# Two-layer decoder trunk on one core: the order of work at the changes of stage is rewritten

## The reference

```python
for l in range(DEPTH):                      # DEPTH = 2
    u = rms_norm(h, norm_pre_mix[l])
    if l == 0: mix = mamba2_mixer(u, ...)   # in_proj, conv, chunked scan, gate, out_proj
    else:      # shared K and V from rms_norm(h, kv_norm_w) @ w_k, w_v, once
               mix = diff_attention(u, k_shared, v_shared, ...)
    h = h + rms_norm(mix, norm_post_mix[l])
    m = sq_relu_mlp(rms_norm(h, norm_pre_mlp[l]), mlp_w1[l], mlp_w2[l])
    h = h + rms_norm(m, norm_post_mlp[l])
return h
```

## Time and profile before

| | us |
|---|---|
| median of 3 runs | 2575.64 (2575.22 to 2575.69) |
| the profiled execution | 2576.61 |
| its span | 2574.9 |
| TensorE busy with matmuls | 2525.8 (98%) |
| VectorE busy | 1796.9 (70%) |
| ScalarE busy | 1212.9 (47%) |
| mean granted TensorE clock | 0.997 |

### The profile page before, as it was taken

The page is one execution under the profiler, slowest core; times in us unless marked ns, Lnnn a source line. Parts: engine busy times, 40 slices in busy tenths (PEclk is TensorE's granted clock), DMA queues, the critical chain, the costliest instruction groups (busy, mean ns, idle before and its releaser), DMA issues.

```text
span 2574.9 us, 45532 instructions
## 1 busy us (share of the span) xinstructions
PE 2525.8 (98%) x17258; PEld 2324.6 (90%) x17258; DVE 1796.9 (70%) x2563; ACT 1212.9 (47%) x1580; POOL 151.9 (6%) x269
## 2 busy tenths in 40 slices
PE   6999999999999999999999999999999999999997
PEld 6999999999898989999998898998899998989896
DVE  4878777877876566666656877778866666575666
ACT  4555555554554443434434654555544434443433
POOL 2221022202100000000000000000000000000000
PEclk9999999999999999999999999999999999999999
DMA  6665665555556666665666555555565666666664
GB/s 177 197 199 164 199 191 188 179 187 181 187 167 193 189 190 192 185 193 184 196 188 193 174 183 176 175 171 165 170 187 182 197 190 190 188 192 190 189 190 135
DMA packets 266506, 474.13 MB, mean 184 GB/s; under 512 B 16577, under 2 KB 50226, under 8 KB 264626
## 3 DMA queue, kind: packets, MB, share of 16 engines
q1 hardware_dynamic: 263296, 457.76, 58.0%
q0 software_dynamic: 2624, 15.00, 1.8%
q10 hardware_dynamic: 498, 0.18, 0.0%
HBM read 470.70 MB, written 2.19 MB: 184 GB/s over the span
## 4 chain that ended last, share of the span: by engine, by line
PE 95%; DVE 3%; ACT 1%; DMA 1%; issue 0%; POOL 0%; ACTq 0%; DVEq 0%; SPq 0%; POOLq 0%
PE ps L1295 31%; PE ps L1297 30%; PE ps L1296 30%; PE ps L1475 1%; DVE h L974 0%; DVE whl L843 0%; DVE xhl L931 0%; DMA par_rows<-a_conv_b 0%; PE ps L1558 0%; PE ps L1479 0%; PE ps L1413 0%; ACT whl L588 0%; PE ps L1467 0%; DVE y L947 0%; PE ps L1379 0%
## 5 line engine op out<-in xcount | busy, mean ns | idle before, releaser
L843 DVE TENSOR_TENSOR whl<-raw,whl 128x1024 fp32r<-128x1024 f32 x865 | 1073.8, 1241 | 716.8 <-ACT whl L588 705.1
L588 ACT ACTIVATE whl<-raw 128x1024 fp32r<-128x1024 f32 x865 | 916.3, 1060 | 1206.1 <-PE ps L1297 1195.7
L1295 PE MATMUL ps<-xhl,whl 128*128 128x256 f32 (+1 forms) x3600 | 1014.4, 282 | 11.1 <-DVE xhl L931 10.1
L1297 PE MATMUL ps<-xhl,whl 128*128 128x256 f32 (+1 forms) x3600 | 1006.4, 280 | 0.0
L1296 PE MATMUL ps<-xhl,whl 128*128 128x256 f32 (+1 forms) x3600 | 1005.3, 279 | 0.0
L1295 PEld LDWEIGHTS ps<-xhl,whl 128*128 128x128 f32 (+1 forms) x3600 | 677.1, 188 | 16.9 <-DVE xhl L931 11.7
L1296 PEld LDWEIGHTS ps<-xhl,whl 128*128 128x128 f32 (+1 forms) x3600 | 677.3, 188 | 3.1 <-issue 1.9
L1297 PEld LDWEIGHTS ps<-xhl,whl 128*128 128x128 f32 (+1 forms) x3600 | 677.0, 188 | 0.0
L1295 PE MATMUL ps<-whl,bhl 128*128 128x512 f32 x1312 | 511.4, 390 | 0.0
L1296 PE MATMUL ps<-whl,bhl 128*128 128x512 f32 x1312 | 510.8, 389 | 0.0
L1297 PE MATMUL ps<-whl,bhl 128*128 128x512 f32 x1312 | 510.5, 389 | 0.0
(11 more groups left out here) (210 smaller groups left out, 1640.5 us busy)
## 6 DMA issues: line engine op xcount, KB each, us to landing
raw<-mlp_w SPq DMA_DIRECT2D x512, 512.0 KB, 4.2
raw<-a_in_proj SPq DMA_DIRECT2D x161, 512.0 KB, 4.7
raw<-a_out_proj SPq DMA_DIRECT2D x64, 512.0 KB, 4.1
raw<-b_w_q SPq DMA_DIRECT2D x32, 512.0 KB, 3.6
raw<-w_k SPq DMA_DIRECT2D x32, 512.0 KB, 3.7
raw<-w_v SPq DMA_DIRECT2D x32, 512.0 KB, 3.7
raw<-b_out_proj SPq DMA_DIRECT2D x32, 512.0 KB, 3.7
cumb<-cum_scratch POOLq DMA_DIRECT2D x8, 1024.0 KB, 7.5
```

The lines of the kernel that those rows point to most:

```text
L588: sc.activation(whi[:, s.split, lo:lo + SLAB], raw[:, s.raw, :], ACT.Copy).then_inc(hi_ready, 1)
L843: ve.tensor_tensor(out=wlo[:, s.split, lo:lo + SLAB], in0=raw[:, s.raw, :], in1=whi[:, s.split, lo:lo + SLAB].bitcast(F32), op=ALU.subtrac ...
L1295: te.matmul(outs, lh, rh, start=start, stop=False, skip_group_check=True)
L1297: return te.matmul(outs, ll, rh, start=False, stop=stop, skip_group_check=True)
```

## The change

The last slab of a stage reports its first half of tokens separately (`half_done`), and VectorE adds that half while TensorE still works on the other. The third block of y is weighed one half of the tokens at a time, the first half ahead of the norm factor, the second later. The first 256 columns of h are renewed as two pieces of 128. TensorE transposes one tile instead of four before the first slab, runs the products with the high half of x as soon as ScalarE has it (`first_slab`), and transposes the later pairs one by one, each ahead of or in the middle of a slab (`x_slab`). ScalarE takes pair 2+i ahead of the split of step i. VectorE takes pairs 1 to 3 inside `boundary`, between parts of `residual`, and pairs 4 to 7 in the steps 0 to 3, with the last block of y and the last piece of h in step 1. The keys' halves move to the steps 0, 1, 4, 5 and 6. ScalarE's squares keep their steps, 3 and 4 (6 and 7 in attention).

The constants:

```diff
-TURN_BANKS = (3, 4, 5, 6, 2, 7, 3, 4)
-H_PIECES = ((0, 256), (256, 512), (512, 1024), (1024, 1536), (1536, 2048))
+TURN_BANKS = ((3, 7), (4, 4), (5, 5), (6, 6), (2, 2), (7, 7), (3, 3), (4, 4))
+H_PIECES = ((0, 128), (128, 256), (256, 512), (512, 1024), (1024, 1536), (1536, 2048))
+X_PIECE = ((0, 1), (2, 2), (3, 3), (3, 3), (4, 4), (4, 4), (5, 5), (5, 5))
+    XK_TURNS = {0: (0,), 1: (1,), 4: (2, 3), 5: (4, 5), 6: (6, 7)}
```

ScalarE's parts:

```diff
+            def x_first(r, col):
+
+                act.wait_ge(xt_first, r)
+                x_tile(0, 0, TURN_BANKS[0], xhi, col).then_inc(x_first_hi, 1)
+                act.wait_ge(xt_done, KT // 2 * r + 1)
+                x_tile(0, 1, TURN_BANKS[0], xhi, col).then_inc(x_hi, 1)
...
                     ahead = ph.slab(first_k + k + LEAD, t, per)
+                    if early:
+                        early(unit, i)
...
                 def first_step(unit, i):
-                    if unit == "up" and i < 3:
-                        x_halves(r, range(2 * i + 2, 2 * i + 4), col)
                     if unit == "up" and i in (3, 4):
                         act.wait_ge(h_new, H_STEPS * r)
                         square_sums(r, range(4 * (i - 3), 4 * (i - 2)))
...
+                def first_turns(unit, i):
+                    if unit == "up" and i < 6:
+                        x_halves(r, (2 + i,), col)
...
-                steps(ph, 0, MLP_FIRST, first_step)
+                steps(ph, 0, MLP_FIRST, first_step, early=first_turns)
```

VectorE's parts:

```diff
             def last_output(ph, r, i):
...
                 for t, done in enumerate((half_added, acc_added)):
+                    if t == 0:
+                        dve.wait_ge(half_done, r + 1)
+                    else:
+                        dve.wait_ge(slab_used, ph.slab(ph.slabs - 1).used)
...
-            def boundary(r, slab=None, col=0):
-
-                weigh_y(r, 2)
+            def post_norm(r):
+
+                weigh_y(r, 2, (0,))
                 dve.wait_ge(y_sq, MT * NT * (r + 1))
                 link(ve.reduce_sum(sum_y, ssy, AX))
                 inverse_rms(rsy, sum_y, D, 1e-6)
+
+            def boundary(r, slab, col):
+
+                post_norm(r)
                 residual(r, 0)
                 residual(r, 1)
-                if slab:
-                    x_halves(r + 1, range(2), col)
+                dve.wait_ge(x_first_hi, r + 1)
+                x_tile(0, 0, TURN_BANKS[0], xhi, xlo, col).then_inc(x_first_lo, 1)
                 residual(r, 2)
-                if slab:
-                    split(slab)
-                residual(r, 3)
+                dve.wait_ge(x_hi, KT // 2 * (r + 1) + 1)
+                x_tile(0, 1, TURN_BANKS[0], xhi, xlo, col).then_inc(x_lo, 1)
+                residual(r, 3, (0,))
+                x_halves(r + 1, (1,), col)
+                residual(r, 3, (1,))
+                split(slab)
+                x_halves(r + 1, (2,), col)
+                weigh_y(r, 2, (1,))
+                residual(r, 4, (0,))
+                x_halves(r + 1, (3,), col)
+                residual(r, 4, (1,))
+
+            def later_pieces(r, i, col):
+
+                if i < 4:
+                    x_halves(r + 1, (4 + i,), col)
+                if i == 1:
+                    weigh_y(r, 3)
+                    residual(r, 5)
+
+            def last_norm(r):
+
+                post_norm(r)
+                for n in range(4):
+                    residual(r, n)
+                weigh_y(r, 2, (1,))
+                residual(r, 4)
                 weigh_y(r, 3)
-                residual(r, 4)
+                residual(r, 5)
...
                 def first_step(unit, i):
-                    if unit == "up" and i < 3:
-                        x_halves(r, range(2 * i + 2, 2 * i + 4), col)
+                    if unit == "up":
+                        later_pieces(r - 1, i, col)
...
             def att_step(first, g, unit, i):
                 if first and unit == "q":
-                    if i < 3:
-                        x_halves(2, range(2 * i + 2, 2 * i + 4), 16)
-                    for j in {0: (0, 1), 3: (2, 3), 4: (4, 5), 5: (6, 7)}.get(i, ()):
+                    for j in XK_TURNS.get(i, ()):
                         dve.wait_ge(xk_hi, j + 1)
                         x_half(j, TURN_BANKS[j], khi, klo, 64, xk_lo)
+                    later_pieces(1, i, 16)
```

TensorE's parts:

```diff
+            def first_slab(r, s):
+
+                transpose_x(r, 0)
+                pe.wait_ge(lo_ready, s.n + 1)
+                wh, wl = slot(s, 2)
+                outs = [ps[:, f // 2, f % 2 * S:(f % 2 + 1) * S] for f in range(4)]
+                cols = [slice(f * P, (f + 1) * P) for f in range(4)]
+                pe.wait_ge(x_first_hi, r)
+                for f in range(4):
+                    te.matmul(outs[f], wh[:, 0, cols[f]], xhi[:, 0, :], start=f % 2 == 0, stop=False, skip_group_check=True)
+                    te.matmul(outs[f], wl[:, 0, cols[f]], xhi[:, 0, :], start=False, stop=False, skip_group_check=True)
+                transpose_x(r, 1)
+                pe.wait_ge(x_first_lo, r)
+                for f in range(4):
+                    te.matmul(outs[f], wh[:, 0, cols[f]], xlo[:, 0, :], start=False, stop=False, skip_group_check=True)
+                pe.wait_ge(x_lo, KT // 2 * r + 1)
+                for f in range(4):
+                    last = three(outs[f], (wh[:, 1, cols[f]], wl[:, 1, cols[f]]), (xhi[:, 1, :], xlo[:, 1, :]), start=False, stop=False)
+                last.then_inc(slab_used, 1)
+
+            def x_slab(r, i, s):
+
+                turn = {1: 0, 5: 1}.get(i)
+
+                def between(f):
+                    if f == turn:
+                        transpose_x(r, i + 1)
+
+                if turn is None and i < 7:
+                    transpose_x(r, i + 1)
+                pe.wait_ge(x_lo, KT // 2 * r + i + 1)
+                feature_major(s, i, (0, 1), (xhi, xlo), between=between)
```

More of the change, by code:

```diff
@@ L599, in square_sums, with x_tile, x_half @@
                     square_sum(n % (2 * MT), h[:, t, piece(p)], ssh[:, t, p:p + 1], h_sq)
[L601 to L607, removed]
+            def x_tile(i, j, banks, dst, col):
+                k = 2 * i + j
+                return sc.activation(dst[:, k, :], ps[:, banks[j], j * S:(j + 1) * S], ACT.Copy, scale=par[:, col + k:col + k + 1])
+            def x_half(i, banks, dst, col, done):
+                x_tile(i, 0, banks, dst, col)
+                x_tile(i, 1, banks, dst, col).then_inc(done, 1)
+            def x_first(r, col):
[3 more added lines that the diff above has]
+                x_tile(0, 1, TURN_BANKS[0], xhi, col).then_inc(x_hi, 1)
             def x_halves(r, tiles, col):
@@ L826, in att_step, with first_turns @@
                     attend(i + 8 * (unit == "out2"), g, LAST_PLAN)
-            x_halves(2, range(2), 16)
+            def first_turns(unit, i):
+                if unit == "q" and i < 6:
+                    x_halves(2, (2 + i,), 16)
+            x_first(2, 16)
+            x_halves(2, (1,), 16)
             for g in range(QG):
-                steps(att, ATT_STARTS[g], ATT[g], lambda u, i: att_step(g == 0, g, u, i))
+                steps(att, ATT_STARTS[g], ATT[g], lambda u, i: att_step(g == 0, g, u, i), early=first_turns if g == 0 else None)
             steps(att, ATT_STARTS[QG], ACC, lambda u, i: output_norm(att, 2, i), urgent=True)
@@ L925, in inverse_rms_of_h, with x_tile, x_half @@
                 inverse_rms(rsh, sum_h, D, 1e-6)
[L927 to L934, removed]
+            def x_tile(i, j, banks, hi, lo, col):
+                k = 2 * i + j
+                return ve.scalar_tensor_tensor(
+                    out=lo[:, k, :], in0=ps[:, banks[j], j * S:(j + 1) * S], scalar=par[:, col + k:col + k + 1],
+                    in1=hi[:, k, :].bitcast(F32), op0=ALU.mult, op1=ALU.subtract)
+            def x_half(i, banks, hi, lo, col, done):
+                x_tile(i, 0, banks, hi, lo, col)
+                x_tile(i, 1, banks, hi, lo, col).then_inc(done, 1)
             def x_halves(r, tiles, col):
@@ L1300, in slot, with feature_major @@
                 return [t[:, s.split, lo:lo + SLAB].rearrange("p (t n) -> p t n", t=tiles) for t in (whi, wlo)]
-            def feature_major(s, i, banks, x, tiles=2, cols=BLK, half=0, last_i=7):
+            def feature_major(s, i, banks, x, tiles=2, cols=BLK, half=0, last_i=7, between=None):
                 pe.wait_ge(lo_ready, s.n + 1)
@@ L1313, in feature_major, with token_major @@
                                      start=(k == 0 and f % 2 + half == 0), stop=(i == last_i and j == tiles - 1))
+                    if between:
+                        between(f)
                 last.then_inc(slab_used, 1)
-            def token_major(s, i, slabs, bank, x, tiles=2, cols=BLK, lo=0):
+            def token_major(s, i, slabs, bank, x, tiles=2, cols=BLK, lo=0, half=False):
                 pe.wait_ge(lo_ready, s.n + 1)
@@ L1329, in token_major @@
```

(25 more changed lines are left out.)

71 lines of the change are left out of this document (37 added, 34 removed).

## The result

The changed kernel takes 2584.03 us (median of 7 runs, 2582.71 to 2586.85), the kernel before 2575.74 (7 runs, 2575.22 to 2577.19). The ratio is 1.0034, 95% interval 1.0022 to 1.0045: 8.3 us slower. 7.4 us had been forecast, to 2583.0. The profiled execution took 2585.17 us with a span of 2583.5, for 2574.9 before.

A forecast was written before the change was run, and what follows sets the result against it. TensorE's weight stream was taken as the bound nearly everywhere, so only stage changes and the end counted: 0.8 + 3.9 + 1.5 + 1.0 + 0.2 = 7.4 us slower, median 2575.64 to 2583.0, range 2581 to 2585.

The forecast's parts named there:

- The front: Start of a stage change: first matmul of slab 0 5.6 us after the output's end (8.0 before), slab 0 ending 1.7 us sooner.
- All of h: First change of stage: the last piece of h, queued on VectorE behind pair 5, completes h at 739.36, 5.0 us after slab 3.
- Slabs 6 and 7: First change: ScalarE's squares stand ahead of pairs 6 and 7, so TensorE waits 1.9 us, then another 1.5 us.
- The first change: First change of stage: spreading of the norm at 753.84 for 753.06, a loss of 0.8 us.
- the third: Third change of stage: like the first, but the early half brings 0.3 us and not 0.6; 1.0 us lost.
- The second change: Second change: VectorE's queue delays the last `klo` to 1473.87; TensorE waits 5.6 us ahead of slab 8, 3.9 us lost.
- The clock behind it: After the second change's long wait: matmuls at half rate over about 3 us lose 1.5 us, which may be 0.
- The end: After the last stage: norm 0.85 us sooner, half weighing and two more residuals added; 0.2 us slower, bounds -0.3 and +0.5.
- (b): Rival: waits ahead of slab 7 at first and third change each followed by half clock, 1.5 us each, 2586.0; chance 0.08.
- (a): Rival: no clock drop after the second change's long wait; 5.9 us slower, 2581.5; chance 0.14.
- (c): Rival: only the keys' wait bites, 2575.6, or only the squares bite, 2575.8; chance 0.12 together.
- (d): Rival: fronts' gain kept through all eight slabs, spreading 2.8 us earlier at each change, 2567.4; chance 0.06.

The follow-up runs named there:

- squares by pieces: Changed kernel with ScalarE's eight squares of h made two in step 2, four in step 3, two in step 5; 2577.67 us, ratio 1.0008.
- filler: Changed kernel with TensorE turning the identity 40 times within the long wait ahead of slab 8 at the second change; 2581.63 us, ratio 1.0022.
- the two single repairs: Two kernels, each the changed kernel with one repair: squares by pieces, 2577.67 us, and keys' new order, 2576.83 us.
- keys' old steps: Changed kernel with the keys' pairs 2 to 7 in steps 3, 4 and 5 as in the kernel before; 2580.74 us, ratio 1.0021.
- keys' new order: Changed kernel with keys' halves ordered 0, 1, 6, 7, 2, 3, 4, 5, ScalarE's steps to match and TensorE's one wait split in five; 2576.83 us.
- half of y early: Kernel before, first half of y's last block added early, third block weighed half ahead of norm, half behind split; 2577.96 us, ratio 1.0007.

## Why the prediction was right

Its steps against the profile after:

- **The front**: first products 5.6 us after the output's end, measured 5.72, 5.61 and 5.89. Right.
- **All of h** at 24.1 us after it, measured 24.4 (739.21 less 714.83). **Slabs 6 and 7**: waits of 1.9 and 1.5 us, measured 1.79 and 1.19 at the third change; at the first, 1.78, and half clock filled the second wait. The first change lost 1.15 us for 0.8, the third 1.02 for 1.0. Of the missing 0.35 us at the first, 0.18 stands ahead of slab 7 (33.05 us after the output's end for 32.87), the rest behind it, where half clock lasted until about 748.3. The squares by pieces showed that ScalarE's squares are the cause and VectorE's queue is not.
- **The second change**: slab 8 3.9 us later. Measured 38.72 less 34.81 (14.06 ahead of 48.87), 3.9. The wait was 5.38 us for 5.6.
- **The clock behind it** was mis-sized. 1.5 us was taken from the start's stretch of 3 us at half clock. It cost 54.92 less 38.72 less 14.06, 2.1 us, since the clock stayed low over 3.8 us of matmuls, and the filler's run measured the same 2.08. In the kernel with squares by pieces it cost 2.6 us behind the same wait.
- **The end**: 0.2 us, measured 0.40, inside the bounds. VectorE was idle for 0.29 us between the norm and the first residual, which the prediction did not have.
- **The sum**: 7.4 us, 8.6 in the profiles and 8.3 in the medians. The five terms came out as 1.15, 3.9, 2.1, 1.02 and 0.40 us. None lies clearly below its forecast, so the nearness of the sum is not one of errors that cancel.
- **The rule of the Trainium skill** (TensorE: Matmul & The Clock Gate, What's actually happening), that an idle array falls back to half rate: it held for the waits of 5.38 and 2.55 us. The prediction took it without regard to how long a wait is, so that a drop would follow each new wait. The trace after agrees at the first change, at slab 6, and disagrees at the third, where 1.79 and 1.19 us cost no clock. The drop at slab 6 came one wait earlier than rival (b) had it, and it was nearly free, since slab 7 was waiting for ScalarE in any case: from the start of slab 6 to that of slab 7 it is 4.26 us at the first change and at the third.

Of the rivals, (a) and (b) concern the clock and are settled above. (c) is refuted by the two single repairs, each of which takes back only its own part. (d), the faster outcome, was a true picture of what the front is worth: the first and third change take 2.3 to 2.5 us less than before once the squares are out of the way, where 2.8 was worked out. It failed at the point named, pair 6 on VectorE by 741.8; VectorE began on it only at 742.69 and was done at 743.57, in a trace that runs 0.4 us ahead of that of the kernel before.

## What to carry to other kernels

When work that came in batches is made to come one piece at a time, go through each in-order engine's list again from the first moved instruction to the first wait that needs all pieces; what stood behind the batch may now stand ahead of the last pieces. Ask of each moved piece which queue will be late last, not which wait it removes, because a gain ahead of a full queue turns into a longer wait (1.57 us became 2.31 here), and half clock can follow such a wait. Where an engine must wait some microseconds anyway, let it wait for a part, do harmless work on what is free, and wait for the rest.

## What the runs showed of the hardware that was not expected

A fallen clock cost 2.1 us behind a wait of 5.38 us, 2.6 us behind one of 5.39 us (squares by pieces) and 1.6 us behind one of 2.55 us, more than the 1.5 us taken from the start.

For waits of about 2 us the length alone does not tell whether the clock falls. Half clock followed the 1.78 us ahead of slab 6 at the first change. It did not follow the same wait at the third change, nor in the kernels with the keys' old steps, with the filler and with the keys' new order, seven waits of 1.77 to 1.79 us. In the kernel with half of y early it followed 2.31 us and did not follow 2.30 and 2.32 us. What decides it no run shows.

The changed kernel's seven runs are spread over 4.1 us and those of the kernel before beside them over 2.0. In the sets of 21 to 33 runs the kernel before is itself spread over 2.8 to 4.0 us, so this difference says little, and whether drops that come and go make the spread was not tested.

Four instructions of 128x128 held VectorE 1.14 us, 0.285 each, where the line through 256 and 512 columns had given 0.27.
